# Gate and up weights read in 8,192-byte runs, with the gathered columns of x taken at a step of four

## The reference

```python
a = jnp.einsum('td,edf->etf', t, w_gate)          # 16 experts, w_gate, w_up: 2048 x 512
u = jnp.einsum('td,edf->etf', t, w_up)
hidden = jax.nn.silu(a) * u * gates.T.astype(t.dtype)[..., None]
out = jnp.einsum('etf,efd->td', hidden, w_down)   # w_down: 512 x 2048
```

## Time and profile before

| | us |
|---|---|
| runs | 2277.85, 2279.94, 2280.59 |
| median | 2279.94 |
| span of the profiled execution, first to last instruction | 2278.6 |
| TensorE busy, matmuls | 2158.8 (95%) |
| weight loads, beside the matmuls | 1310.8 (58%) |
| VectorE busy | 863.4 (38%) |
| ScalarE busy | 399.3 (18%) |

### The profile page before, as it was taken

The page is one execution under the profiler, slowest core; times in us unless marked ns, Lnnn a source line. Parts: engine busy times, 40 slices in busy tenths (PEclk is TensorE's granted clock), DMA queues, the critical chain, the costliest instruction groups (busy, mean ns, idle before and its releaser), DMA issues.

```text
span 2278.6 us, 28323 instructions
## 1 busy us (share of the span) xinstructions
PE 2158.8 (95%) x10618; PEld 1310.8 (58%) x10619; DVE 863.4 (38%) x1565; ACT 399.3 (18%) x726; POOL 16.4 (1%) x105
## 2 busy tenths in 40 slices
PE   7999999899899999999799999998998999999996
PEld 3678867684554444555347788576745554444552
DVE  1134555552533223322511435555515333223325
ACT  0103220100321122211101032201103221122211
POOL 2000000000000000000000000000000000000000
PEclk9999999999899999999989999999998999999998
DMA  6433332105699999999534333321057999999993
GB/s 222 142 108 130 112 130 74 56 20 203 252 385 392 397 398 396 394 396 397 202 118 152 107 129 112 129 75 56 1 203 291 391 396 392 397 397 397 395 395 122
DMA packets 227050, 539.02 MB, mean 237 GB/s; under 512 B 15824, under 2 KB 20368, under 8 KB 209296
## 3 DMA queue, kind: packets, MB, share of 16 engines
q1 hardware_dynamic: 226960, 537.83, 64.1%
HBM read 535.70 MB, written 2.10 MB: 236 GB/s over the span
## 4 chain that ended last, share of the span: by engine, by line
PE 90%; DVE 6%; issue 3%; ACT 1%; DMA 0%; POOL 0%; DVEq 0%; ACTq 0%; POOLq 0%
PE bank L1034 19%; PE bank L685 16%; PE bank L674 15%; PE bank L1073 10%; PE bank L993 5%; PE bank L1005 3%; PE bank L1055 3%; PE bank L1007 2%; PE bank L709 2%; PE bank L895 2%; PE bank L907 2%; PE bank L904 2%; DVE mix_acc L1762 1%; DVE v_rot L1467 1%; PE bank L618 1%
## 5 line engine op out<-in xcount | busy, mean ns | idle before, releaser
L674 PE MATMUL bank<-x_t,ring 128*128 128x256 f32 x1536 | 351.2, 385 | 0.0
L674 PEld LDWEIGHTS bank<-x_t,ring 128*128 128x128 f32 x1536 | 288.6, 191 | 55.0 <-issue 18.2
L685 PE MATMUL bank<-ring,x_t 128*128 128x512 f32 (+1 forms) x640 | 256.1, 554 | 4.4 <-DVE x_t L1354 4.4
L1034 PE MATMUL bank<-ring,region_a 128*64 128x512 f32 x1024 | 231.4, 594 | 0.0
L1766 DVE COPY region_a<-bank 128x512 f32<-128x512 f32 x32 | 22.1, 692 | 496.8 <-PE bank L1034 496.8
L685 PEld LDWEIGHTS bank<-ring,x_t 128*128 128x128 f32 x640 | 120.3, 192 | 118.8 <-issue 115.5
L685 PE MATMUL bank<-ring,mix_acc 128*128 128x512 f32 x384 | 174.9, 593 | 1.5 <-ACT mix_acc L1242 1.5
L1762 DVE TENSOR_TENSOR mix_acc<-bank,mix_acc 128x512 f32<-128x512 f32 x272 | 165.8, 681 | 1.9 <-PE bank L1007 1.6
L1005 PE MATMUL bank<-y_hi,scat_rows 128*128 128x512 f32 x272 | 113.7, 418 | 43.0 <-DVE mix_acc L1762 39.8
L1034 PEld LDWEIGHTS bank<-ring,region_a 128*64 128x64 f32 x1024 | 72.2, 137 | 138.9 <-issue 137.0
L1781 DVE SCALAR_TENSOR_TENSOR y_lo<-bank,slot_gate,y_hi 128x512 fp32r<-128x512 f32 x128 | 96.1, 751 | 124.8 <-ACT y_hi L1303 115.4
(11 more groups left out here) (339 smaller groups left out, 2160.1 us busy)
## 6 DMA issues: line engine op xcount, KB each, us to landing
ring<-in_w_gate_dram SPq DMA_DIRECT2D x128, 1024.0 KB, 9.9
ring<-in_w_in_dram SPq DMA_DIRECT2D x80, 1024.0 KB, 5.0
ring<-in_w_up_dram SPq DMA_DIRECT2D x64, 1024.0 KB, 13.0
region_b<-in_w_up_dram SPq DMA_DIRECT2D x64, 1024.0 KB, 14.1
x_t<-in_w_down_dram SPq DMA_DIRECT2D x64, 1024.0 KB, 10.2
ring<-in_w_out_dram SPq DMA_DIRECT2D x32, 1024.0 KB, 5.2
region_b<-in_w_down_dram SPq DMA_DIRECT2D x32, 1024.0 KB, 7.2
conv_sq<-in_w_down_dram SPq DMA_DIRECT2D x32, 1024.0 KB, 9.3
```

What stands on the lines that cost most here:

```text
L674: m = pe.matmul(b[c // 2][:, (c % 2) * T:(c % 2 + 1) * T], w[:, kk, c * P:(c + 1) * P], xT[:, k, :], start=(k == 0 and c % 2 == 0), stop=( ...
L685: m = pe.matmul(b[t][:, 0:width], lhs[:, k, t * P:(t + 1) * P], w[:, kk, 0:width], start=(k == 0), stop=(k == KC - 1))
L1034: m = pe.matmul(bank[2 + w][side * SLOTS:(side + 1) * SLOTS, :], xg_half[k // 8][:, k % 8 * P + slots.start:k % 8 * P + slots.stop], exp_s ...
```

## The change

The gate and up weights are seen with the 2,048 rows split as (j, p, k), k the innermost of four. Piece j still holds the rows 512j to 512j + 511, but partition p now has the four neighbouring rows 512j + 4p to 512j + 4p + 3, which are one run of 8,192 bytes in memory. The four chunks of a piece then hold the rows 512j + 4q + k. So the gather takes for chunk 4b + j the columns 512b + 4q + j of `x_nat`, q from 0 to 127, by the view `x_rows`: 128 columns at a step of four words. Names aside, the loops, waits, banks and slots are the old ones, and the down weights are loaded as before.

```diff
--- before.py
+++ after.py
@@ -152,6 +152,7 @@
 
         ring = sb("ring", [P, RING, PIECE])
         x_nat = sb("x_nat", [P, NT, D])
+        x_rows = x_nat[:, :, :].rearrange("p t (j q k) -> p t j k q", q=P, k=4)
         x_t = sb("x_t", [P, KC * T])
         xT = x_t[:, :].rearrange("p (c t) -> p c t", c=KC)
         mix_acc = sb("mix_acc", [P, KC * T])
@@ -410,8 +411,8 @@
 
         w_in_v = w_in.rearrange("l (k p) n -> l p k n", p=P)
         w_out_v = w_out.rearrange("l (k p) n -> l p k n", p=P)
-        w_gate_v = w_gate.rearrange("l e (k p) f -> (l e) p k f", p=P)
-        w_up_v = w_up.rearrange("l e (k p) f -> (l e) p k f", p=P)
+        w_gate_v = w_gate.rearrange("l e (j p k) f -> (l e) p j (k f)", p=P, k=4)
+        w_up_v = w_up.rearrange("l e (j p k) f -> (l e) p j (k f)", p=P, k=4)
         w_down_v = w_down.rearrange("l e (f p) d -> (l e) p f d", p=P)
 
         def piece(n):
@@ -544,8 +545,7 @@
                     dst = exp_slot[j]
                     if j < 8:
                         w = (w_gate_v, w_up_v)[j // 4]
-                        dst = dst.rearrange("p (k n) -> p k n", k=4)
-                        src = w[bass.ds(le, 1), :, 4 * (j % 4):4 * (j % 4) + 4, :].rearrange("a p k f -> (a p) k f")
+                        src = w[bass.ds(le, 1), :, j % 4, :].rearrange("a p f -> (a p) f")
                     else:
                         src = w_down_v[bass.ds(le, 1), :, j - 8, :].rearrange("a p d -> (a p) d")
                     sp.dma_start(dst, src).then_inc(landed[j].sem, 16)
@@ -989,9 +989,8 @@
                     for b in range(4):
                         for j in range(4):
                             for t in range(NT):
-                                c = 4 * b + j
                                 m = pe.matmul(bank[GATHER_BANKS[b]][:, j * P:(j + 1) * P],
-                                              x_nat[:, t, c * P:(c + 1) * P], pick2[:, t, :],
+                                              x_rows[:, t, b, j, :], pick2[:, t, :],
                                               start=(t == 0), stop=(t == NT - 1))
                         m.then_inc(gather_done.sem, 1)
```

## The result

The changed kernel takes 2397.99 us (median, 2397.21 to 2398.97) against 2279.8 us: a ratio of 1.052, 95% interval 1.0505 to 1.0535, so 118 us slower. The span of the profiled execution went from 2278.6 to 2395.4 us, by 116.8.

A forecast was written before the change was run, and what follows sets the result against it. TensorE was taken to set the end, with DMA slightly ahead. Transfers at zero plus 102.7 us for the gather's stepped load, on the 2278.6 us span, gave 2381.3, and 1.3 to the median made 2383 us; range 2276 to 2420 us.

The forecast's parts named there:

- What bounds the kernel: Expert stages: TensorE sets the end at 31.8 us a turn; DMA runs a little ahead, 31.7 us of transfer.
- the 7.6 us of room: Expert turns: the last up piece lands by 778.1 us and is needed from 785.7 us on.
- The transfers at zero: Gate and up pieces: transfer falls from 21.7 to 19.9 us a turn, hidden under TensorE's matmuls, costed at zero.
- the up pieces' issue time would fall: SyncE's issue of an up piece: from a median 1243 ns to near a down piece's 352 ns.
- The count of packets: Gate and up transfers: packets should fall by three quarters of 131,072.
- The load is exposed: Gather: pairs go at the load's pace, 114.7 ns, so a longer load lengthens the chain one for one.
- The size of the term: Gather's load with a step of four: 215 ns a pair instead of 114.7, times 1024 pairs, +102.7 us.
- The half-clock row: Trace row at granted clock 0.50: two 128-column load pairs at 215 ns each, taken as the stepped load's price.
- The upper bound: Gather's load: one fetch a word where four shared one, four times 114.7 ns, +352 us over 1024 pairs.
- A, the free step: Rival, gather: the stepped load takes no longer and the DMA gain is hidden; 2280 us, chance 0.29.
- B, a load more than 2.2 times as long: Rival, gather: a far slower load, up to four times; 2420 to 2632 us, chance 0.14.
- C, the weights' arrival: Rival, expert turns: weights' arrival binds, so long runs save 58 us; 2222 us at best, chance 0.03.

The follow-up runs named there:

- wide gathers: Both masks as one 256-column moving operand per gather matmul: changed kernel (step of four) 2405.03 us, kernel before (adjacent columns) 2383.94 us.
- half gather: Kernel before with only the first tile's tokens gathered, 32 pairs instead of 64: 2246.91 us with 2,048-byte weight runs, 2222.47 us with 8,192-byte runs.

## Why the prediction was right

**What bounds the kernel.** Right. TensorE's chain had no wait on DMA, and the long runs alone gave a ratio of 1.0001. The working was even close at the next step: with TensorE taken down to 30.0 us a turn, the old runs settled at 31.6 us a turn against 31.7 worked out. One reading in it was wrong: the 7.6 us of room count the last issue's 2.0 us twice and take the slowest landing, and the trace has 11.6 there.

**The transfers at zero.** Right, with the cover that it named (TensorE's own 31.8 us a turn). Where that cover was taken away, the price appeared: 24 us. The underrated room changed nothing in the sum. That the up pieces' issue time would fall was borne out, but it was a weaker sign than the prediction made it: with the old runs and the longer turns the median falls to 373 ns as well. The count of packets, 98,305 fewer, is the sign that only the runs can give.

**The load is exposed.** Right. That the fold's pairs had the same pace with half of the moving columns was the reading on which this rested. The wide gathers confirm it from the other side: behind 256 moving columns most of the step's price is gone.

**The size of the term.** The mechanism was right and the size was low. The prediction took 215 ns a pair from the load at half clock, +102.7 us. The pair took 236.4 ns, 121.7 more than before, and the gather grew by 7.79 us where 6.4 (64 x 100.3 ns) had been worked out. Over 14 gathers that is 14 x 7.79 = 109.1 us; the two first gathers of the layers grew only from 10.05 to 15.20 and from 10.37 to 15.20, by 5.2 and 4.8 us; in all 119.0 us, of which 116.8 arrive in the span. The missing 2.2 us lie outside of the gathers (1.0 of them ahead of the first one, which starts at 607.33 instead of 608.35) and weren't followed up. That the first gathers would grow less had been said. The half-clock row was near, but by luck: it is a load bound by the engine's clock, and this one is bound by what it fetches and hardly feels the clock. Nor does the price go in whole steps, as the reason for the row had it: steps of two and three words give 120.9 and 178.1 ns. The range says little, as it held no change at all beside the forecast; what speaks for the working is that the gather grew and, within the expert stages, nothing else.

**The upper bound.** It assumed that four adjacent words share one fetch and that fetches bind already. The first is what the steps show, the second is not: 32 pieces at 1.80 ns would be 63 ns with the rule's 5.4, well under the 114.7 of adjacent columns. The load of adjacent words is bound by its columns (the pair goes from 114.7 to 215 ns at half clock), and by the rule nearly twice its 32 pieces could be fetched in its time ((114.7 - 5.4) / 1.80 = 61). So the price is a factor of two and not of four.

**The rivals.** A, the free step, is out by every kernel with a step of three words or more. B, a load more than 2.2 times as long, is out: it is 2.06 times. C, the weights' arrival, is out in both kernels. It is real in the half gather with the old runs, where a turn took what the rates say once the room was used up (31.6 us).

Of the pages that the prediction weighed, the Trainium skill's SBUF — State Buffer ("Door 1: The DMA port swizzle") tells of 16-byte lines and of two hits a line for full bandwidth. The steps agree: that of two, with two hits, made the pair 5% longer, that of three 55% and that of four 106%. Its example, that a step of four fp32 words is free, is not borne out. The pairs of adjacent words that the Trainium skill's Vector Engine (DVE) Microarchitecture Reference (section 5.2) asks for on VectorE are not what TensorE's load asks for, since the step of two has no adjacent words and runs nearly at the full rate. The formula of the Trainium skill's TensorE: Matmul & The Clock Gate ("LDWEIGHTS (loading the stationary operand)"), by columns alone, comes within 8 ns of the pair of adjacent words (106.7 against 114.7) and near that of a step of two, and misses that of a step of four by 130 ns.

No kernel here beats the one before in the full work. The long runs could be had with adjacent columns if `x_nat` were stored in the order of the weights once a layer; as TensorE sets the end, the kernel with long runs alone shows what this could give at most, nothing measurable, and it wasn't tried.

## What to carry to other kernels

When a weight layout is changed for longer runs, the other operand pays: look where its step ends up, and whether that read has cover. By the runs here, a stationary operand of float32 should take at least two words out of every 16 bytes, or stand beside a matmul at least as long as the stepped load. And a resource that looks full is worth speeding up only if someone waits for it. Here the DMA engines showed 9 tenths at 395 GB/s before, and again 9 tenths at some 350 with the step alone. The chain and the waits tell, and taking some of the other engine's work away shows what the reserve would be worth.

## What was unexpected of the hardware

The load's time follows the number of 16-byte pieces touched, in proportion: 120.9, 178.1 and 236.4 ns a pair for 64, 96 and 128, some 1.80 ns apiece; adjacent words (32 pieces) stay at 114.7. The granted clock shows only where the columns take longer than the pieces: steps of two and three fall to the same 14 pairs in 3 us at clock 0.50, while the gather with a step of four takes 15.20 us at a mean of 0.82 and 15.13 at 1.00. With one piece a word the distance matters little and not in order: steps of 4, 8 and 16 words gave gathers of 15.13, 15.43 and 14.17 us.
